# Softmax weights turned by a matmul with a diagonal of reciprocal sums

## The reference, cut to what matters

```python
# moba_attention: 8 heads of width 64; with 256 tokens there is one block, so it is causal softmax attention
s_own = jnp.where(kpos_own[None, :] <= qpos[:, None], s_own, NEG)
p = jax.nn.softmax(jnp.concatenate([s_past, s_own], axis=-1), axis=-1).astype(v.dtype)
...
# causal_block_attention: 8 heads in each of the 2 layers of the second network
s = jnp.where(kpos[None, :] <= qpos[:, None], s, -jnp.inf)
...
# dilated_group_attention, in 3 groups of dilation (1, 4, 16) of 8 heads, in each of those 2 layers
lse = jax.nn.logsumexp(s, axis=-1)
p = jnp.exp(s - lse[..., None])
o = jnp.einsum('bdhnqk,bdhnkc->bdhnqc', p, vw)
...
# hybrid_layer: the three groups are weighted by a softmax over their lse, which makes one softmax of all three
alpha = jax.nn.softmax(jnp.stack(lses, axis=0), axis=0)
o_c = jnp.sum(alpha[..., None] * jnp.stack(outs, axis=0), axis=0)
```

## Time and profile before

| | us |
|---|---|
| median of 3 runs | 1436.99 (1436.65 to 1437.37) |
| profiled execution, its own time | 1437.06 |
| its span, first to last instruction | 1435.3 |
| TensorE busy | 1417.0, 99% |
| VectorE busy | 1040.7, 73% |
| ScalarE busy | 857.3, 60% |

### The profile page before, as it was taken

How to read it: one execution, slowest core, us unless ns; L and a number is a source line. 1 busy time by engine, 2 the same in 40 slices (tenths; PEclk the granted TensorE clock), 3 DMA queues, 4 the chain that set the end, 5 groups by cost and what they waited for, 6 DMA issues and landing times.

```text
span 1435.3 us, 30487 instructions
## 1 busy us (share of the span) xinstructions
PE 1417.0 (99%) x11812; PEld 1332.8 (93%) x11812; DVE 1040.7 (73%) x1782; ACT 857.3 (60%) x1482; POOL 92.0 (6%) x148
## 2 busy tenths in 40 slices
PE   8999999999999999999999999999999999999999
PEld 5888999999989999999998989989999898989999
DVE  2888899887785677865675857886677685787664
ACT  4466666655556666445566776565566686655553
POOL 0101011110000000000001000220000100031000
PEclk9999999999999999999999999999999999999999
DMA  9966699997674465766663555346666355534663
GB/s 363 339 207 219 232 332 334 337 361 233 204 233 152 154 193 180 237 198 191 192 231 115 173 158 159 117 128 196 192 194 225 105 175 164 160 104 139 188 204 118
DMA packets 81122, 291.93 MB, mean 203 GB/s; under 512 B 9185, under 2 KB 10465, under 8 KB 80882
## 3 DMA queue, kind: packets, MB, share of 16 engines
q1 hardware_dynamic: 68274, 244.31, 52.6%
q0 software_dynamic: 12304, 45.26, 9.4%
q10 hardware_dynamic: 432, 0.79, 0.2%
HBM read 289.27 MB, written 1.05 MB: 202 GB/s over the span
## 4 chain that ended last, share of the span: by engine, by line
PE 84%; DVE 9%; ACT 4%; issue 3%; DMA 0%; SPq 0%; DVEq 0%; ACTq 0%
PE G L549 21%; PE G L550 20%; PE G L551 20%; DVE wlo L1800 3%; PE G L608 3%; PE G L610 3%; PE G L609 3%; ACT whi L1257 1%; PE Tp L1097 1%; PE S L1069 1%; DVE sn L2430 1%; PE Tp L728 1%; PE Tp L1083 1%; PE G L630 1%; PE S L697 1%
## 5 line engine op out<-in xcount | busy, mean ns | idle before, releaser
L1800 DVE TENSOR_TENSOR wlo<-raw,whi 128x1024 fp32r<-128x1024 f32 x442 | 541.3, 1227 | 250.0 <-ACT whi L1257 248.1
L1257 ACT ACTIVATE whi<-raw 128x1024 fp32r<-128x1024 f32 x442 | 466.8, 1058 | 206.2 <-PE G L551 150.4
L549 PE MATMUL G<-h,whi 128*128 128x256 f32 x2064 | 581.5, 282 | 2.3 <-DVE at L2480 1.9
L550 PE MATMUL G<-h,whi 128*128 128x256 f32 x2064 | 571.3, 277 | 0.0
L551 PE MATMUL G<-h,wlo 128*128 128x256 f32 x2064 | 571.3, 277 | 0.0
L549 PEld LDWEIGHTS G<-h,whi 128*128 128x128 f32 x2064 | 388.0, 188 | 12.6 <-issue 8.4
L550 PEld LDWEIGHTS G<-h,whi 128*128 128x128 f32 x2064 | 387.8, 188 | 0.7 <-issue 0.5
L551 PEld LDWEIGHTS G<-h,wlo 128*128 128x128 f32 x2064 | 387.8, 188 | 0.0
L1808 DVE CUSTOM_DVE_ANT_0 aw<-aw,cs,cols 128x1024 f32<-128x1024 f32 x80 | 101.4, 1279 | 0.0
L549 PE MATMUL G<-ah,whi 128*128 128x256 f32 x352 | 97.2, 276 | 0.0
L550 PE MATMUL G<-ah,whi 128*128 128x256 f32 x352 | 97.2, 276 | 0.0
(11 more groups left out here) (442 smaller groups left out, 2315.3 us busy)
## 6 DMA issues: line engine op xcount, KB each, us to landing
raw<-in_w SPq DMA_DIRECT2D x444, 512.0 KB, 3.8
aw<-in_ada POOLq DMA_DIRECT2D x80, 512.0 KB, 5.2
adaw<-in_ada SPq DMA_DIRECT2D x8, 1024.0 KB, 15.3
sn<-in_uq POOLq DMA_DIRECT2D x2, 768.0 KB, 5.2
x<-in_x SPq DMA_DIRECT2D x1, 1024.0 KB, 5.4
pt<-in_ukv POOLq DMA_DIRECT2D x2, 512.0 KB, 6.8
out<-x SPq DMA_DIRECT2D x4, 256.0 KB, 2.2
dec<-in_dec ACTq DMA_DIRECT2D x1, 512.0 KB, 10.0
```

What stands on the lines that cost most here:

```text
L549: pe.matmul(o, wh, mv[:, 0:T], start=(k == 0), stop=False)
L550: pe.matmul(o, wh, mv[:, T:2 * T], start=False, stop=False)
L1257: act.activation(whi[:, s, :], raw[:, s, :], ACT.Copy).then_inc(w_hi, 1)
L1800: dve.tensor_tensor(wlo[:, s, :], raw[:, s, :], whi[:, s, :], ALU.subtract).then_inc(w_lo, 1)
```

## The change: what it does

VectorE no longer multiplies the weights. It writes a diagonal instead: `on_diagonal` multiplies the identity, read twice, by the two columns of reciprocals, each spread over 128 columns, in one `tensor_tensor` of 128x256. The result is two diagonal matrices side by side, one for each half of the queries, in `rtmp` (first network) or in `sq[:, 4:6]` (second). TensorE's transposes become `pe.matmul` with the unscaled weights stationary and the diagonal of that half of the queries moving, which turns and scales in one. The operands have the same sizes as those of the transposes, and the order of the work, the semaphores and the buffers of scores, weights and PSUM stay. For each head one VectorE instruction takes the place of two; on TensorE 168 transposes (24 + 48 + 96) become 168 fp32 matmuls.

```diff
--- before.py
+++ after.py
@@ -779,11 +779,13 @@
                 if odd:
                     ins.then_inc(o_done, 1)
 
-            def transposes_p(src):
+            def transposes_p(src, weight):
 
                 slot = use_t()
                 for j in range(3):
-                    ins = pe.transpose(Tp[:, slot, j * P:(j + 1) * P], src[:, j * P:(j + 1) * P], ident[:, :])
+                    qt = 1 if j else 0
+                    ins = pe.matmul(Tp[:, slot, j * P:(j + 1) * P], src[:, j * P:(j + 1) * P], weight[:, P * qt:P * qt + P],
+                                    start=True, stop=True)
                 ins.then_inc(t_done, 1)
 
 
@@ -867,7 +869,7 @@
                     moba_scores(i)
                 if 1 <= i <= 8:
                     pe.wait_ge(pn_ready, i)
-                    transposes_p(pr[:, (i - 1) % 2, :])
+                    transposes_p(pr[:, (i - 1) % 2, :], rtmp[:, (i - 1) % 2, :])
                 if b in (15, 17, 19, 21):
                     sb_scores(b - 15)
                     sb_scores(b - 14)
@@ -996,10 +998,13 @@
                     pe.wait_ge(t_free, freed)
                     return slot
 
-                def to_keys(src, at_cols):
+                def to_keys(i, at_cols):
                     slot = use_t()
+                    src, weight, first = sn[:, i % 2, :], sq[:, 4 + i % 2, :], spans(i)[0].stop
                     for j, c in enumerate(at_cols):
-                        ins = pe.transpose(Tp[:, slot, j * P:(j + 1) * P], src[:, c:c + P], ident[:, :])
+                        qt = 0 if c < first else 1
+                        ins = pe.matmul(Tp[:, slot, j * P:(j + 1) * P], src[:, c:c + P], weight[:, P * qt:P * qt + P],
+                                        start=True, stop=True)
                     ins.then_inc(t_done, 1)
 
                 def block1(j):
@@ -1171,7 +1176,7 @@
                 def third_group(i):
 
                     if i > 8:
-                        to_keys(sn[:, (i - 1) % 2, :], WEIGHT_TILES[1])
+                        to_keys(i - 1, WEIGHT_TILES[1])
 
                 def pair_outs(p):
 
@@ -1221,7 +1226,7 @@
                     if i >= 1:
                         pe.wait_ge(weights_ready, l * 16 + i)
                         for tiles in ((0, P, 2 * P),) if i <= 8 else WEIGHT_TILES if i == 16 else WEIGHT_TILES[:1]:
-                            to_keys(sn[:, (i - 1) % 2, :], tiles)
+                            to_keys(i - 1, tiles)
 
 
                 for mm in range(4):
@@ -1920,12 +1925,16 @@
                                                    accum_out=mn[:, i % 2, qt:qt + 1])
                 ins.then_inc(s_free, 1)
 
+            def on_diagonal(dve, to, weights):
+
+                return dve.tensor_tensor(to.rearrange("p (q c) -> p q c", q=2), ident[:, :].unsqueeze(1).broadcast_to([P, 2, P]),
+                                         weights.unsqueeze(2).broadcast_to([P, 2, P]), ALU.mult)
+
             def moba_normalise(i):
                 s = i % 2
                 dve.wait_ge(p_ready, i + 1)
                 chain.link(dve.reciprocal(ri[:, s, :], rs[:, s, :]))
-                dve.tensor_scalar(pr[:, s, 0:P], pr[:, s, 0:P], ri[:, s, 0:1], None, ALU.mult)
-                dve.tensor_scalar(pr[:, s, P:384], pr[:, s, P:384], ri[:, s, 1:2], None, ALU.mult).then_inc(pn_ready, 1)
+                on_diagonal(dve, rtmp[:, s, :], ri[:, s, :]).then_inc(pn_ready, 1)
 
             dve.wait_ge(cs_copied, 1)
             for b in range(25):
@@ -2443,9 +2452,7 @@
                     s = i % 2
                     dve.wait_ge(p_ready, 8 + l * 16 + i + 1)
                     chain.link(dve.reciprocal(rj[:, s, :], rs2[:, s, :]))
-                    for qt, r in enumerate(spans(i)):
-                        ins = dve.tensor_scalar(sn[:, s, r], sn[:, s, r], rj[:, s, qt:qt + 1], None, ALU.mult)
-                    ins.then_inc(weights_ready, 1)
+                    on_diagonal(dve, sq[:, 4 + s, :], rj[:, s, :]).then_inc(weights_ready, 1)
 
                 y_n = [0]
```

## The result

| median of the runs, us | before | after | ratio (95% interval) |
|---|---|---|---|
| first comparison | 1437.18 (1436.65 to 1438.61) | 1454.96 (1451.42 to 1455.81) | 1.0117 (1.0105 to 1.0130) |
| changed kernel again, second chip | 1436.92 | 1454.05 | 1.0108 (1.0077 to 1.0140) |
| changed kernel again, third chip | 1437.30 | 1453.44 | 1.0107 (1.0091 to 1.0122) |

A forecast was written before the change was run, and what follows sets the result against it. TensorE, busy 99% of the span, was taken as the bound: 1437.06 + 18.6 for turns - 5.3 for waits = 1450.4 us, median 1450.3 us, 0.9% slower; 8-in-10 range 1446.5 to 1457.5 us.

The forecast's parts named there:

- The price of a turn: TensorE, 168 turns: fp32 matmul leaves two records, 0.22 us against 0.11 for a transpose; 18.6 us more in all.
- The waits of L786 and L858: TensorE's weight-load waits around the first network's turns: 1.1 us gained at L786, 0.5 us at L858.
- only VectorE's 0.13 us is gained: L786, first network: the turn stands in the loop, so each of eight waits shortens by 0.13 us, 1.1 us.
- L2480 and L1002: TensorE's waits in the second network, 2.4 us and 1.3 us; both were to go entirely.
- VectorE's 1.0 us and TensorE's 2.0 us: At L2480: VectorE arrives at least 1.0 us earlier, TensorE 2.0 us later, so the 2.4 us wait goes.
- Rival 1: The waits don't pay: TensorE gets its 18.6 us, VectorE waits for scores; 1455.6 us, up to 1458; 22%.
- 2 us on each side: Allowance for fp32r matmul blocks running at 0.113 or 0.118 us spacing, which the prediction couldn't derive.
- Rival 2: The second record costs nothing, a turn still takes 0.11 us; only VectorE's relief is left, 1433 us; 4%.
- Rival 3: The turn is four times dearer on TensorE: 168 x 0.33 = 55 us, 1487 us with the waits; 2%.
- Rival 4: New waits: ScalarE, held by later turns, gives `whi` late; at most 13 us more, 1464 us; 5%.
- The stretch of 76 us: Window from 880 to 956 us, to become about 76 + 8.0 - 1.8 = 82 us.
- A stretch without softmax changes by more than 1 us: One of the prediction's signs that it is wrong, to be read in the changed profile.

The follow-up runs named there:

- diagonal alone: Kernel before with VectorE writing diagonals, weights left unscaled, identity transposes kept, division by the sums left out; 1433.08 us, 0.9972.
- the matmuls alone: Kernel before with the 168 transposes as fp32 matmuls with the identity, VectorE scaling as before; 1453.67 us, 1.0106, and 1454.37 us, 1.0111.

## Why the prediction was right, and where its size was off

*The price of a turn.* The mechanism is right: 336 records, and no new wait of TensorE in A, B or C. The size was a little too low. Between the start of the matmul ahead and that of the third one behind, at places without a wait, three tiles take 0.34 us more in the second network (0.33 forecast) and 0.38 us more in the first; six take 0.68 us more between blocks (0.67 forecast) and 0.73 us more behind products with the values. That is 8 x 0.38 + 16 x 0.34 + 16 x 0.70 = 19.7 us instead of 18.6. The prediction had 18.0 to 19.8 as bounds and took one distance for all records. What it left out is the start of a group: behind products with the values, and in the first network, the first distance is 0.213 us against 0.165 for a transpose. That is 0.05 us for each of 16 groups, 0.8 us; the rest is 0.112 us in place of 0.111.

*The waits of L786 and L858.* 1.1 and 0.5 us were to be gained. The pool of the first network has gone from 1.5 + 1.4 + 0.8 = 3.7 us to 2.8 us, so it was 0.9 us. What failed is "only VectorE's 0.13 us is gained" as a gain at each of eight waits: diagonal alone, with the turns as before, shortened these waits by 0.2 us in all (2.9 to 2.6 before the turns, 0.8 to 0.9 for L858). TensorE's lateness doesn't shorten them by much either: the matmuls alone leave 3.6 and 3.3 of the 3.7 us in their two profiles. Only with both parts is it 2.8 to 3.2 us, in all four profiles that have them in the first network. With the rise by 3.0 us (8 x 0.38) A comes out: +3.0 - 0.9 = +2.1 us, measured +2.1 (2.1 to 2.6 over three profiles, forecast 1.1). How the two parts share the 0.9 us is open.

*L2480 and L1002.* Both waits are gone, 3.7 us, as forecast. The working counted VectorE's 1.0 us and TensorE's 2.0 us towards them; against 1.2 us in each layer the 2.0 us are enough alone, and the matmuls alone show it. So the waits gained are nearly the same whether VectorE saves anything or not, 3.8 and 4.1 us with its old work and 4.2 to 4.6 us with the new.

*Waits together.* 7.4 - 2.8 = 4.6 us were gained, 5.3 forecast. Rival 1 had nothing gained. Its time of 1455.6 us is nearer to all three medians (0.6 to 2.2 us off) than the forecast's 1450.3 (3.1 to 4.7 us off), but its account is refuted: in the second network the turns cost 8.4 us more in each layer, and B and C grew by only 6.4 to 7.0 us. It comes near because the 4.6 us of waits are nearly made up for by the 1.1 us that the turns cost more and by the 1 to 2.7 us that no term had. Its other half, that VectorE's gain turns into waits for scores, is borne out: beside the long turns that gain can't be told from nothing.

*The balance of the profiled executions.* 19.7 of turns, less 4.6 of waits, and 0.3 us for three more runs on the slow spacing in B and C (16, where this profile of before has 13) make 15.4 us; A, B and C grew by 15.2 us. The span grew by 14.3 us only, since M took 2.1 us more, the stretch between B and C 1.1 us less, and the ends of the program 1.9 us less. The other executions of the first comparison are 3 us longer. No trace of them is there; the two later profiles, at 1452.0 and 1452.9 us, have 0.7 and 0.4 us of their surplus in B and C and the rest spread over the program, 0.7 and 1.5 us of it before A. The part of the 16 to 18 us that is not turns less waits is 1 to 2.7 us. About 0.9 us of it is the slower spacing beside fp32 turns, for which the prediction had kept 2 us on each side without a direction; the rest isn't placed. So the range held because it reached over that allowance and over rival 1, and not because every term was right; that the result lies inside it is partly luck.

*VectorE.* The new instruction takes 0.43 us (0.42 forecast), and VectorE is busy 7.4 us less in all (9). It waits longer for scores, as forecast: within one layer, for `sn` from TensorE's issue, 3.9 us in five waits before and 7.8 us in nine after. From VectorE's waits between 878 and 970 us in the changed kernel:

```profile
DVE sn L2439 <- issue: 7.8, 9, 1.4
...
DVE at L2490 <- ACT at L1739: 3.9, 2, 2.3
```

*Rivals 2, 3 and 4.* Rival 2 (the second record free) asked for less than 0.024 us for each; it is 0.117 us (19.7 / 168). Rival 3 (0.33 us more for each turn) is refuted by the same number. The Trainium skill ("TensorE: Matmul & The Clock Gate", Terms) has the transpose mode 4x faster for fp32; this trace has it 2x faster at 128 columns, and an fp32r matmul of the same size just as fast. Rival 4 had TensorE wait for `whi`; its waits in A, B and C name none.

*What the profile was to show.* The records, 0.83 and 1.5 us, 40 instructions on VectorE, the lost wait and the chain on TensorE from 907 to 955 us are all there. The stretch of 76 us was to grow by 6.2 us; B and C, which hold the same work, have grown by 6.4 to 7.0 us. The first network's was to grow by about 1 us, and A has grown by 2.1 to 2.6 us. "A stretch without softmax changes by more than 1 us" was a bad test: M changed by 2.1 us, and by 1.6 us without any change to the kernel.

## What to carry to other kernels

On a kernel where TensorE bounds, count the records of a matmul's data type before work is moved to it. Here a true fp32 matmul was two, an fp32r matmul or a transpose one, and the same idea was 16 to 18 us slower with the first and 3.7 to 5.0 us faster with the second, where the softmax weights are kept as fp32r alone. Two edits that both shorten the same wait are not worth the sum of what each is worth alone; read the second one's worth from the waits that are left when the first is in. Profile the unchanged kernel twice before a difference of 1 or 2 us in a far stretch is put down to a change.

## What was new about the hardware

Back-to-back fp32r matmuls with 256 moving columns run at 0.113 or 0.118 us each for a whole run of them, at the full granted clock, and a run can change between two executions of one kernel (288 matmuls: 32.6 or 33.9 us). The slower one is more frequent beside true fp32 matmuls, 8 to 12 of 19 runs against 4 to 7 beside transposes. Inside the stretches with turns it can be seen at 24 matmuls; this is one block of the changed kernel, 15 matmuls in 1.77 us, 0.118 us each:

```profile
886.17 0.28 PE L551 MATMUL G<-h,wlo 128*128 128x256 f32 x1
...
887.94 0.28 PE L551 MATMUL G<-h,wlo 128*128 128x256 f32 x1
```

True fp32 records of 128 columns follow one another at 0.112 us and transposes at 0.109 us, wherever they stand. Behind products with the values the first distance alone is longer, 0.213 us for fp32 and 0.165 us for a transpose. A weight load for a transpose lasts 0.14 us and one for a true fp32 or an fp32r matmul 0.19 us. The longer load shows no cost by itself: with fp32r the first distance is 0.163 us and three turns took no longer than three transposes.
